# Three of four weight differences move from VectorE to GpSimd in the last feed-forward stage

## The chip, the cores and the metric

The kernel runs on one core of one Trainium2 chip. The metric is the device time of one execution in microseconds (us), the lower the better. It is taken several times, and the median counts.

## The reference, cut to what matters

The reference is a trunk of two layers over 512 tokens of width 1024, in f32. Each layer has a mixer (attention and two gated recurrences), cross-attention to a memory, and a gated feed-forward stage. Only the feed-forward stage of the second layer is touched by the change:

```python
def conv_glu_ffn(h_norm, w_in, conv_w, conv_b, w_out):
    gate, up = jnp.split(h_norm @ w_in, 2, axis=-1)   # w_in is 1024 x 5632
    ...                                               # causal conv of width 3 over the tokens of gate
    return (jax.nn.silu(conv) * up) @ w_out           # w_out is 2816 x 1024
```

## The kernel before

All products keep f32 accuracy by splitting both operands into a high and a low half (`hi` = the value rounded to fp32r, `lo` = the value minus `hi`), and by three matmuls for each product: hi x hi, hi x lo, lo x hi.

**Slabs.** Weights arrive as slabs of 128 x 1024 f32 (512 KB) in a ring of three raw buffers, loaded by SyncE's DMA queue in the order of use. ScalarE writes `w_hi` (L1356). The low half `w_lo` is made in one of three ways: a subtraction on GpSimd (L691), a subtraction on VectorE (`out_low`, L1940, for the slabs of the output product), or, for most `up` slabs of the last feed-forward stage, ScalarE writes the negated rounded slab into `w_lo` (L1355) and a DMA issued by GpSimd (L681) adds the raw slab onto it. `w_hi` and `w_lo` have three buffers each, so that slab k can be split only once TensorE has finished slab k-3. A raw buffer is loaded again once its slab's low half is made (SyncE waits for that).

**The last feed-forward stage.** The 22 chunks of 128 hidden columns come in three groups g of 8, 8 and 6 (`LG`). For each chunk c TensorE multiplies the slab `("gate", g, c)` and then the slab `("up", g, c)`, 24 matmuls each. VectorE takes them out of the banks (L2232 for gate, L2241 for up), does the convolution (L2234, L2236, L2237), multiplies (L2243), and prepares operands for the output product (L1947 to L1958). ScalarE does the SiLU (L1707) and high halves (L1714, L1719, L1722). ScalarE splits slabs two ahead: only after the high halves of chunk c (`pair_high_halves`) does it split the gate slab of chunk c+2, and then the up slab of chunk c+2.

**The output product** behind each group is Strassen's form with seven half-size products, which need four sums of the activations and four differences of quarters of the weights. The quarters `b11`, `b12`, `b22`, `b21` of `w_out` are loaded whole during the chunks, and the differences are

- `t1 = b12 - b11`, `t2 = b22 - t1`, `t3 = b22 - b12`, `t4 = b21 - t2`.

Each is one subtraction per slab of 128 x 1024 (two slabs per group; the second slab of the last group is 128 x 512): 24 subtractions in all, all on VectorE, at L1933 in `t_sum`. `T_CHUNK` says behind which chunk: for group 0 `t1`, `t2`, `t3` behind chunks 4, 5, 6, for group 1 behind 3, 4, 5, for group 2 behind 2, 3, 4. `t4` comes later. `t1` and `b21` of group 0 are written over `h`, so that they wait for semaphore `hk_evac` to reach 8, when ScalarE (L1737) has copied `h`, transposed, out of the banks in eight pieces; it does the last four of these copies in chunk 4, behind its split of the slabs of chunk 5.

**GpSimd's queue** in this stage holds, slab by slab in the order of use, the subtraction for each gate slab (L691) and the DMA for each up slab (L681; `added` leaves out only the first two up slabs of group 0 and the first of the others). It waits for nothing else:

```python
if gi in dma_los:
    pool.wait_ge(S["negated"], added.index(gi) + 1)
    pool.dma_start(w_lo[gi % SPLIT][:, 0:n], raw[ring_of[gi] % RAW][:, 0:n], accum_op=ALU.add
                   ).then_inc(lo_in[dma_los[gi][0]], 16)
    continue
```

TensorE's `use` of an up slab waits for that DMA's semaphore `lo_in`.

Of the kernel before, what the change touches and what calls it, by code (L numbers as in the profile page):

```python
# [27 lines left out]
def build_trunk(nc, A, out):  # L28
# [8 lines left out]
    ACT, ALU, AX = mybir.ActivationFunctionType, mybir.AluOpType, mybir.AxisListType  # L37
# [165 lines left out]
    def pair_slabs(g):  # L203

        return [(s, min(2, LG[g] // 2 - 2 * s)) for s in range((LG[g] // 2 + 1) // 2)]
# [19 lines left out]
    def slab_of(layer, name):  # L225
        return first_slab[layer] + layer_at[layer][name]
# [21 lines left out]

    def t_count(g, name, s):

        return sum(len(T_AT) * len(pair_slabs(j)) for j in range(g)) + T_AT[name] * len(pair_slabs(g)) + s + 1

    with ExitStack() as ctx:

# [107 lines left out]
        def b_slab(name, s, nk):  # L362
# [25 lines left out]
            proj_mm h_added mem_r memT_mm m_hi_done m_lo_done ckv_mm ckv_evac ck_ss ck_r ck_done ckT_mm ckT_evac  # L388
            cq_mm cq_evac cq_ss cq_r cqT_mm cqT_evac
            ffn_mm gate_ready sg_done sg_scaled cig_half silu_done act_ready a_hi_done a_lo_done first_rest_in first_hi zeroed qx_done q_scaled  # L390
            p_hi_done p_lo_done sums_done t_done out_lo out_mm c_added
            nope_in sq_done tab_done kr_done constants_made bounds_done pos_in logits_in mix_rows_in rows_in pairs_made  angles_done tables_done""".split()
        S = {n: ctx.enter_context(nc.semaphore(n)) for n in names}
        raw_in = [ctx.enter_context(nc.semaphore(f"raw_in{i}")) for i in range(RAW)]
# [107 lines left out]
        with nc.Block() as block:  # L502
# [121 lines left out]
            def recurrences(pool, layer):  # L624
# [15 lines left out]
                for n in range(NT):  # L640
                    sg = sg_tok[:, n, :].rearrange("p (m h x) -> p m h x", m=2, x=64)
                    pool.tensor_tensor(sg, sg, spread[:, g0:g0 + 128].rearrange("p (m x) -> p m x", m=2).unsqueeze(2)
                                       .to_broadcast([P, 2, NH, 64]), ALU.mult).then_inc(S["sg_scaled"], 1)

            @block.gpsimd
            def _(pool):
                link = chain(pool, S["chain_p"])
# [26 lines left out]
                for layer in range(DEPTH):  # L674
                    for i, (nk, cols, src) in enumerate(layer_slabs[layer]):
# [9 lines left out]
                        if gi == 0:  # L685
# [4 lines left out]
                        pool.wait_ge(S["hi_split"], gi + 1)  # L690
                        pool.tensor_tensor(w_lo[gi % SPLIT][:, c0:n], whole[:, c0:n],  # L691
                                           w_hi[gi % SPLIT][:, c0:n].bitcast(f32), ALU.subtract).then_inc(S["lo_split"], 1)
                        if 2 <= gi < 2 + len(LEVELS):
                            pairs_of(gi - 2)
                        if i == SPLIT - 1:
# [618 lines left out]
            def _(act_):  # L1314
# [20 lines left out]
                for layer in range(DEPTH):  # L1335
                    def split_through(i):

                        while nsplit[0] <= min(i, len(flat) - 1):
                            k = nsplit[0]
                            nk, cols, src = flat[k]  # L1340
                            n = nk * cols
                            if k in ring_of:
                                whole = raw[ring_of[k] % RAW][:, 0:n]
                                act_.wait_ge(raw_in[ring_of[k] % RAW], arrivals[k])
                            else:
                                name, g, s = src
                                whole = b_slab(name, s, nk)
                                if name in T_AT:
                                    act_.wait_ge(S["t_done"], t_count(g, name, s))
                                else:  # L1350
                                    act_.wait_ge(b_in[name], b_loads(g))
                            if k >= SPLIT:
                                act_.wait_ge(*released[k - SPLIT])
                            if k in dma_los:
                                act_.activation(w_lo[k % SPLIT][:, 0:n], whole, ACT.Copy, scale=-1.0).then_inc(S["negated"], 1)  # L1355
                            act_.activation(w_hi[k % SPLIT][:, 0:n], whole, ACT.Copy).then_inc(S["hi_split"], 1)  # L1356
                            nsplit[0] += 1
# [410 lines left out]
            def _(dve):  # L1768
# [50 lines left out]
                for layer in range(DEPTH):  # L1819
# [90 lines left out]
                    def b_ready(g, name):  # L1910
                        dve.wait_ge(b_in[name], b_loads(g))

                    def t_sum(g, name, s, nk):

                        if name == "t1":
                            b_ready(g, "b11")
                            b_ready(g, "b12")
                            if g == 0:
                                dve.wait_ge(S["hk_evac"], 2 * NT)
                            plus, minus = "b12", "b11"  # L1920
                        if name == "t2":
                            b_ready(g, "b22")
                            dve.wait_ge(S["t_done"], t_count(g, "t1", s))
                            plus, minus = "b22", "t1"
                        if name == "t3":
                            dve.wait_ge(S["t_done"], t_count(g, "t1", s))
                            plus, minus = "b22", "b12"
                        if name == "t4":
                            b_ready(g, "b21")
                            dve.wait_ge(S["out_lo"], out_los[slab_of(layer, ("out", g, 0, s))])  # L1930
                            dve.wait_ge(S["t_done"], t_count(g, "t2", s))
                            plus, minus = "b21", "t2"
                        dve.tensor_tensor(b_slab(name, s, nk), b_slab(plus, s, nk), b_slab(minus, s, nk), ALU.subtract  # L1933
                                          ).then_inc(S["t_done"], 1)

                    def out_low(g, q, s, nk):

# [28 lines left out]
                    def out_stage(g):  # L1966

                        some = pair_slabs(g)
                        for q in range(len(PRODUCTS)):
                            add_product(g, q)  # L1970
                            if q + 2 < len(PRODUCTS):
                                for s, nk in some:
                                    out_low(g, q + 2, s, nk)
                            if q == 0:
                                for s, nk in some[1:]:
                                    t_sum(g, "t4", s, nk)

                    link(dve.tensor_scalar(lb_floor[:, :], lb_all[:, :, layer:layer + 1].squeeze(2), 1.0, None, ALU.mult))
                    link(dve.tensor_scalar(lb_rest[:, :], lb_floor[:, :], -1.0, 1.0, ALU.mult, ALU.add))
# [265 lines left out]
                    if layer == LAST:  # L2245
                        for g in range(len(LG)):
                            for c in range(LG[g]):
                                n = LG_FIRST[g] + c
                                some = pair_slabs(g)

                                def second_slab_low():
                                    for s, nk in some[1:]:
                                        out_low(g, 0, s, nk)

                                if c < LG[g] - 1:
                                    glu_chunk(n, 2 * (n % 2))
                                else:
                                    glu_chunk(n, 2 * (n % 2), second_slab_low)
                                pair_operands(g, c)
                                if c in T_CHUNK[g]:  # L2260
                                    for s, nk in some:
                                        t_sum(g, T_CHUNK[g][c], s, nk)
                                if c == LG[g] - 2:
                                    out_low(g, 0, *some[0])
                                    t_sum(g, "t4", *some[0])
                            out_stage(g)
                        continue

# [36 lines left out]
```

## Time and profile before

| | |
|---|---|
| median of 3 runs | 1407.16 us (1406.26 to 1407.54) |
| the profiled execution's own time | 1407.03 us |
| its span, first to last instruction | 1405.2 us |
| granted TensorE clock, mean | 0.996 |
| TensorE busy | 1386.0 us (99% of the span) |
| VectorE busy | 850.2 us (61%) |
| ScalarE busy | 666.1 us (47%) |
| GpSimd busy | 588.3 us (42%) |
| last feed-forward stage, chunks and output products | from about 1060 us of the span to its end |

The span leaves out 1.8 us of the execution's own time. Times in the trace's views are microseconds from the start of the span. In a list of instructions in order of time a row is: start, duration, engine, line, operation, output and inputs with shapes, count, and in brackets how long the engine had been idle and for whom it waited. PE is TensorE, DVE VectorE, ACT ScalarE, POOL GpSimd.

### The profile page before, as it was taken

Reading aid. Unit: us, or ns where it says so; the run is one execution under the profiler, and the core shown is the slowest. Engines: PE = TensorE matmul, PEld = TensorE weight load, DVE = VectorE, ACT = ScalarE, POOL = GpSimd, SP = SyncE. Lnnn points to the kernel's source line nnn. Section 1 sums busy time; section 2 is a strip of 40 time slices with the busy share of each in tenths; the row PEclk is TensorE's granted clock in tenths of the full one; section 3 lists DMA queues with packets and bytes.
Section 4 is the critical chain, followed back from the end, with each engine's and each line's share of the span. In section 5 each row is a group of like instructions: output and inputs, shape, how many; then the busy total and the mean of one; then the engine's idle time right before and its main releaser. Section 6 shows DMA issues by size and latency. Waiting matters only on the chain. (4 is left out here: it accounts for less than half of the span.)

```text
span 1405.2 us, 17641 instructions
## 1 busy us (share of the span) xinstructions
PE 1386.0 (99%) x6797; PEld 1137.1 (81%) x6797; DVE 850.2 (61%) x1267; ACT 666.1 (47%) x1127; POOL 588.3 (42%) x347
## 2 busy tenths in 40 slices
PE   8999999999999999999999999999999999999998
PEld 6888778887788888888888887788878878888887
DVE  4584675565775305664164656746657695598487
ACT  6747482655432212233256465736655443444333
POOL 5645663552444444444445457635423202220320
PEclk9999999999999999999999999999999999999999
DMA  6332012331243333332333220123326626651631
GB/s 179 96 100 61 30 37 80 110 108 58 76 119 91 97 98 99 97 105 83 103 96 95 84 76 16 46 75 121 105 57 189 165 53 188 151 126 60 165 90 60
DMA packets 178898, 135.11 MB, mean 96 GB/s; under 512 B 14945, under 2 KB 152960, under 8 KB 178816
## 3 DMA queue, kind: packets, MB, share of 16 engines
q1 hardware_dynamic: 175664, 124.55, 29.9%
q0 software_dynamic: 2592, 9.44, 3.4%
q8 instruction: 54, 0.88, 0.3%
q14 instruction: 28, 0.23, 0.1%
q10 hardware_dynamic: 560, 0.01, 0.0%
HBM read 122.44 MB, written 2.10 MB: 89 GB/s over the span
## 5 line engine op out<-in xcount | busy, mean ns | idle before, releaser
L691 POOL TENSOR_TENSOR w_lo<-raw,w_hi 128x1024 fp32r<-128x1024 f32 (+3 forms) x188 | 451.2, 2404 | 682.1 <-ACT w_hi L1356 680.4
L771 PE MATMUL bank<-x_hi,w_hi 128*128 128x512 f32 x944 | 371.5, 394 | 4.3 <-issue 1.7
L775 PE MATMUL bank<-x_hi,w_lo 128*128 128x512 f32 x944 | 367.5, 389 | 0.0
L773 PE MATMUL bank<-x_lo,w_hi 128*128 128x512 f32 x944 | 367.4, 389 | 0.0
L1356 ACT ACTIVATE w_hi<-raw 128x1024 fp32r<-128x1024 f32 (+2 forms) x205 | 212.8, 1039 | 217.4 <-PE bank L775 212.5
L771 PEld LDWEIGHTS bank<-x_hi,w_hi 128*128 128x128 f32 x944 | 177.2, 188 | 47.8 <-issue 8.6
L773 PEld LDWEIGHTS bank<-x_lo,w_hi 128*128 128x128 f32 x944 | 177.3, 188 | 37.5 <-issue 1.4
L775 PEld LDWEIGHTS bank<-x_hi,w_lo 128*128 128x128 f32 x944 | 177.2, 188 | 37.1
L1889 DVE TENSOR_TENSOR h<-h,bank 128x512 f32<-128x512 f32 x48 | 31.8, 682 | 105.2 <-PE bank L775 105.1
L1707 ACT ACTIVATE conv<-conv 128x512 f32<-128x512 f32 x44 | 27.8, 633 | 137.5 <-DVE conv L2237 137.5
L1822 DVE SCALAR_TENSOR_TENSOR x_lo<-h,gains_all,x_hi 128x512 fp32r<-128x512 f32 x40 | 41.9, 1059 | 64.1 <-ACT x_hi L1373 63.1
L2232 DVE TENSOR_TENSOR gate_in<-bank,r_bc 128x512 f32<-128x512 f32 x44 | 30.3, 689 | 80.5 <-PE bank L775 71.0
L771 PE MATMUL bank<-w_hi,x_hi 128*128 128x512 f32 (+1 forms) x192 | 77.9, 406 | 0.0
L2236 DVE SCALAR_TENSOR_TENSOR conv<-gate_in,gains_all,conv 128x512 f32<-128x512 f32 x44 | 76.6, 1742 | 1.6
L775 PE MATMUL bank<-w_hi,x_lo 128*128 128x512 f32 (+1 forms) x192 | 74.6, 389 | 0.0
L773 PE MATMUL bank<-w_lo,x_hi 128*128 128x512 f32 (+1 forms) x192 | 74.6, 388 | 0.0
L771 PE MATMUL bank<-a_hi,w_hi 128*128 128x512 f32 x176 | 68.5, 389 | 0.0
L773 PE MATMUL bank<-a_lo,w_hi 128*128 128x512 f32 x176 | 68.5, 389 | 0.0
L775 PE MATMUL bank<-a_hi,w_lo 128*128 128x512 f32 x176 | 68.5, 389 | 0.0
L771 PE MATMUL bank<-w_hi,p_hi 128*128 128x512 f32 x154 | 60.1, 390 | 0.9 <-DVE w_lo L1940 0.9
L775 PE MATMUL bank<-w_hi,p_lo 128*128 128x512 f32 x154 | 59.9, 389 | 0.0
L773 PE MATMUL bank<-w_lo,p_hi 128*128 128x512 f32 x154 | 59.9, 389 | 0.0
(343 smaller groups left out, 2482.1 us busy)
## 6 DMA issues: line engine op xcount, KB each, us to landing
raw<-in_w_ffn_in SPq DMA_DIRECT2D x88, 512.0 KB, 3.8
raw<-in_w_in SPq DMA_DIRECT2D x27, 512.0 KB, 3.8
raw<-in_w_ffn_out SPq DMA_DIRECT2D x20, 512.0 KB, 3.7
w_lo<-raw POOLq DMA_DIRECT2D x18, 512.0 KB, 7.0
raw<-in_w_mix_out SPq DMA_DIRECT2D x16, 512.0 KB, 3.9
raw<-in_w_ca_kv SPq DMA_DIRECT2D x32, 256.0 KB, 3.2
raw<-in_w_ca_q SPq DMA_DIRECT2D x8, 512.0 KB, 3.4
raw<-in_w_ca_out SPq DMA_DIRECT2D x8, 512.0 KB, 3.7
```

Of the source, the lines that this page charges most:

```text
L691: pool.tensor_tensor(w_lo[gi % SPLIT][:, c0:n], whole[:, c0:n], w_hi[gi % SPLIT][:, c0:n].bitcast(f32), ALU.subtract).then_inc(S["lo_split ...
L771: pe.matmul(o, ah, bh, start=first, stop=False, skip_group_check=shared_bank)
L773: pe.matmul(o, ah, bl, start=False, stop=False, skip_group_check=shared_bank)
L775: mm = pe.matmul(o, al, bh, start=False, stop=last, skip_group_check=shared_bank)
L1356: act_.activation(w_hi[k % SPLIT][:, 0:n], whole, ACT.Copy).then_inc(S["hi_split"], 1)
L1707: act_.activation(conv[n % 2][:, :], conv[n % 2][:, :], ACT.Silu).then_inc(S["silu_done"], 1)
L1822: dve.scalar_tensor_tensor(x_lo[:, k, :], h[:, k, :], gain_of(layer + w // 3, name, k), x_hi[:, k, :].bitcast(f32), ALU.mult, ALU.subtract ...
L1889: dve.tensor_tensor(h[:, k, :], h[:, k, :], pb[PROJ_BANKS[base // H_ADDS][half][c]][:, :], ALU.add).then_inc(S["h_added"], 1)
L2232: dve.tensor_tensor(gi[:, CONV - 1:], pb[b][:, :], r_bc[:, :], ALU.mult).then_inc(S["gate_ready"], 1)
L2236: link(dve.scalar_tensor_tensor(cv[:, :], gi[:, t:t + SEQ], w_(t), cv[:, :], ALU.mult, ALU.add))
```

## The change

`t1`, `t2` and `t3` are taken out of VectorE's program and put into GpSimd's, in the loop over the slabs, behind the subtraction for the gate slab of the chunk after the one where VectorE did them: for group 0 gate slabs 5, 6, 7, for group 1 gate slabs 4, 5, 6, for group 2 gate slabs 3, 4, 5. They stand ahead of the DMA of the up slab of the same chunk. That is 18 subtractions. `t4` stays on VectorE and has a semaphore of its own, `t4_done`. For groups 1 and 2 `t1` has a new wait, for the last `out_low` of the group before.

```diff
     def t_count(g, name, s):
-        return sum(len(T_AT) * len(pair_slabs(j)) for j in range(g)) + T_AT[name] * len(pair_slabs(g)) + s + 1
+        kinds = 1 if name == "t4" else 3
+        return sum(kinds * len(pair_slabs(j)) for j in range(g)) + T_AT[name] % 3 * len(pair_slabs(g)) + s + 1
...
+            def difference(pool, g, name, s, nk):
+                plus, minus = {"t1": ("b12", "b11"), "t2": ("b22", "t1"), "t3": ("b22", "b12")}[name]
+                if name == "t1":
+                    pool.wait_ge(b_in["b11"], b_loads(g))
+                    pool.wait_ge(b_in["b12"], b_loads(g))
+                    if g:
+                        pool.wait_ge(S["out_lo"], out_los[slab_of(LAST, ("out", g - 1, 6, pair_slabs(g - 1)[-1][0]))])
+                    else:
+                        pool.wait_ge(S["hk_evac"], 2 * NT)
+                else:
+                    pool.wait_ge(b_in["b22"], b_loads(g))
+                    pool.wait_ge(S["t_done"], t_count(g, "t1", s))
+                pool.tensor_tensor(b_slab(name, s, nk), b_slab(plus, s, nk), b_slab(minus, s, nk), ALU.subtract).then_inc(S["t_done"], 1)
...
             def _(pool):
...
                         pool.tensor_tensor(w_lo[gi % SPLIT][:, c0:n], whole[:, c0:n],
                                            w_hi[gi % SPLIT][:, c0:n].bitcast(f32), ALU.subtract).then_inc(S["lo_split"], 1)
+                        if layer == LAST:
+                            for g in range(len(LG)):
+                                for c, name in T_CHUNK[g].items():
+                                    if i == layer_at[LAST]["gate", g, c + 1]:
+                                        for s, nk_b in pair_slabs(g):
+                                            difference(pool, g, name, s, nk_b)
...
                                 pair_operands(g, c)
-                                if c in T_CHUNK[g]:
-                                    for s, nk in some:
-                                        t_sum(g, T_CHUNK[g][c], s, nk)
                                 if c == LG[g] - 2:
                                     out_low(g, 0, *some[0])
-                                    t_sum(g, "t4", *some[0])
+                                    last_difference(g, *some[0])
```

`last_difference` is the `t4` branch of `t_sum`, with `t4_done` in place of `t_done`; ScalarE waits for `t4_done` ahead of the high half of a `t4` slab.

## Rows read from the trace of the kernel before

**Rows 1.** The page: busy time, share of the span and instructions of TensorE and the others.

```profile
PE 1386.0 (99%) x6797; PEld 1137.1 (81%) x6797; DVE 850.2 (61%) x1267; ACT 666.1 (47%) x1127; POOL 588.3 (42%) x347
```

**Rows 2.** Waits of TensorE, 1050 to 1405 (total, times, longest us); last row 1125 to 1130.

```profile
PE bank L771 <- DMA w_lo<-raw: 1.3, 2, 1.0
PE bank L771 <- DVE w_lo L1940: 0.9, 2, 0.6
...
PE bank L771 <- DMA w_lo<-raw: 0.3, 1, 0.3
```

**Rows 3.** Line L1933: VectorE's t1, t2 and t3 (duration ns min/median/max, first and last start).

```profile
L1933 DVE TENSOR_TENSOR h<-b_y,b_x x6: 1211/1217/3439, 1112.3 to 1343.1; 128x1024 f32<-128x1024 f32 x5, 128x512 f32<-128x512 f32 x1
L1933 DVE TENSOR_TENSOR b_u<-b_z,h x6: 679/2318/3437, 1126.2 to 1359.1; 128x1024 f32<-128x1024 f32 x5, 128x512 f32<-128x512 f32 x1
L1933 DVE TENSOR_TENSOR b_y<-b_z,b_y x6: 687/1218/3434, 1135.8 to 1365.9; 128x1024 f32<-128x1024 f32 x5, 128x512 f32<-128x512 f32 x1
```

**Rows 4.** VectorE in order of time: evacuations of gate (L2232) and up (L2241) slabs.

```profile
1104.60 0.69 DVE L2232 TENSOR_TENSOR gate_in<-bank,r_bc 128x512 f32<-128x512 f32 x1 [2.01 <-PE bank L775]
...
1110.04 0.69 DVE L2241 TENSOR_TENSOR act<-bank,r_bc 128x512 f32<-128x512 f32 x1 [2.59 <-PE bank L775]
...
1115.48 0.69 DVE L2232 TENSOR_TENSOR gate_in<-bank,r_bc 128x512 f32<-128x512 f32 x1 [0.84 <-PE bank L775]
...
1214.58 0.69 DVE L2241 TENSOR_TENSOR act<-bank,r_bc 128x512 f32<-128x512 f32 x1 [1.53 <-PE bank L775]
...
1225.46 0.69 DVE L2241 TENSOR_TENSOR act<-bank,r_bc 128x512 f32<-128x512 f32 x1 [2.59 <-PE bank L775]
```

**Rows 5.** GpSimd in order of time: gate slabs 5, 6 of group 0; 4, 5 of group 1.

```profile
1102.30 2.55 POOL L691 TENSOR_TENSOR w_lo<-raw,w_hi 128x1024 fp32r<-128x1024 f32 x1 [9.31 <-ACT w_hi L1356]
1106.10 0.90 POOL L681 DMA_DIRECT2D w_lo<-raw  x1 [1.25 <-ACT w_lo L1355]
1117.57 2.39 POOL L691 TENSOR_TENSOR w_lo<-raw,w_hi 128x1024 fp32r<-128x1024 f32 x1 [10.57 <-ACT w_hi L1356]
1120.48 0.88 POOL L681 DMA_DIRECT2D w_lo<-raw  x1 [0.52 <-ACT w_lo L1355]
...
1217.49 2.38 POOL L691 TENSOR_TENSOR w_lo<-raw,w_hi 128x1024 fp32r<-128x1024 f32 x1 [5.48 <-ACT w_hi L1356]
1221.52 0.88 POOL L681 DMA_DIRECT2D w_lo<-raw  x1 [1.64 <-ACT w_lo L1355]
1230.39 2.56 POOL L691 TENSOR_TENSOR w_lo<-raw,w_hi 128x1024 fp32r<-128x1024 f32 x1 [8.00 <-ACT w_hi L1356]
1232.91 0.86 POOL L681 DMA_DIRECT2D w_lo<-raw  x1
```

**Rows 6.** L681, issue to landing: all 18; then those issued at 1221.5, 1232.9, 1358.0.

```profile
DMA to landing us min/median/max: 4.5/7.0/8.9
...
DMA to landing us min/median/max: 5.6/5.6/5.6
...
DMA to landing us min/median/max: 7.1/7.1/7.1
...
DMA to landing us min/median/max: 4.5/4.5/4.5
```

**Rows 7.** ScalarE in order of time: the last `hk_evac` copies, gate slab 6 of group 0.

```profile
1106.57 2.04 ACT L1737 ACTIVATE h_tok<-bank 128x512 f32<-128x512 f32 x4
...
1116.42 1.06 ACT L1356 ACTIVATE w_hi<-raw 128x1024 fp32r<-128x1024 f32 x1 [4.51 <-DMA raw<-in_w_ffn_in]
```

**Rows 8.** VectorE's convolution step alone, then beside a GpSimd subtraction; both engines near 278.

```profile
1105.91 0.75 DVE L2236 SCALAR_TENSOR_TENSOR conv<-gate_in,gains_all,conv 128x512 f32<-128x512 f32 x1
...
1117.58 2.94 DVE L2237 SCALAR_TENSOR_TENSOR conv<-gate_in,gains_all,conv 128x512 f32<-128x512 f32 x1
...
277.92 6.21 POOL L691 TENSOR_TENSOR w_lo<-raw,w_hi 128x1024 fp32r<-128x1024 f32 x2 [3.08 <-ACT w_hi L1356]
...
278.55 3.31 DVE L1831 TENSOR_TENSOR h_sq<-h_sq 128x1024 f32<-128x1024 f32 x1
```

More of the change, by code:

```diff
@@ L390, in build_trunk @@
             ffn_mm gate_ready sg_done sg_scaled cig_half silu_done act_ready a_hi_done a_lo_done first_rest_in first_hi zeroed qx_done q_scaled
-            p_hi_done p_lo_done sums_done t_done out_lo out_mm c_added
+            p_hi_done p_lo_done sums_done t_done t4_done out_lo out_mm c_added
             nope_in sq_done tab_done kr_done constants_made bounds_done pos_in logits_in mix_rows_in rows_in pairs_made  angles_done tables_done""".split()
@@ L1348, in split_through @@
                                 if name in T_AT:
-                                    act_.wait_ge(S["t_done"], t_count(g, name, s))
+                                    act_.wait_ge(S["t4_done" if name == "t4" else "t_done"], t_count(g, name, s))
                                 else:
@@ L1911, in b_ready, with last_difference @@
                         dve.wait_ge(b_in[name], b_loads(g))
[L1913 to L1934, printed above, removed]
+                    def last_difference(g, s, nk):
+                        b_ready(g, "b21")
+                        dve.wait_ge(S["out_lo"], out_los[slab_of(layer, ("out", g, 0, s))])
+                        dve.wait_ge(S["t_done"], t_count(g, "t2", s))
+                        dve.tensor_tensor(b_slab("t4", s, nk), b_slab("b21", s, nk), b_slab("t2", s, nk), ALU.subtract
+                                          ).then_inc(S["t4_done"], 1)
                     def out_low(g, q, s, nk):
@@ L1975, in out_stage @@
                                 for s, nk in some[1:]:
-                                    t_sum(g, "t4", s, nk)
+                                    last_difference(g, s, nk)
                     link(dve.tensor_scalar(lb_floor[:, :], lb_all[:, :, layer:layer + 1].squeeze(2), 1.0, None, ALU.mult))
```

## The prediction

> **What bounds the kernel now.** I read the page first, for who is busy. TensorE is busy 99% of the span, the other engines 42 to 61% [rows 1], so taking work from VectorE gains only what TensorE now waits for. The waits of TensorE in the last feed-forward stage give the size: 1.3 us for the DMA that makes an up slab's low half, 0.9 us for VectorE's `out_low` [rows 2]. That is 2.2 us in 350. The question is then how much slack the low halves have on the way through GpSimd's queue.
>
> For that I read VectorE, GpSimd and ScalarE in order of time. Each evacuation marks the end of a slab on TensorE: gate slab 4 of group 0 at 1104.6, up slab 4 at 1110.0, gate slab 5 at 1115.5 [rows 4], so a slab takes 5.44 us. GpSimd makes the low half of gate slab 5 at 1102.30 to 1104.85 and issues the DMA for up slab 5 at 1106.10 [rows 5]. Such a DMA lands 4.5 to 8.9 us after issue, median 7.0 [rows 6]. One of the TensorE waits, 0.3 us, stands just where up slab 6 of group 0 begins [rows 2]: this chain already touches TensorE.
>
> **What is removed.** 18 VectorE subtractions. The full ones take 1.21 us undisturbed and up to 3.44 us [rows 3]. VectorE gets 5 to 10 us less per group. The most that this can give back on TensorE is the 0.9 us of waits for `out_low`, of which 0.6 us lie behind the last up slab, at the end of a chain that starts with that slab's own evacuation and holds no t-difference; I take 0.3 us, between 0 and 0.9.
>
> **What is added on GpSimd.** A subtraction of this shape costs 2.39 us there [rows 5]; two make 4.8 us. They stand between the gate slab's subtraction and the up slab's DMA, and the queue is in order, so the DMA moves back by 4.8 us less the time that GpSimd sits idle in between. Behind the DMA waits TensorE. Behind the landing waits also SyncE, which reloads the raw buffer, two slabs further on; that has some 5 us to spare and is costed at nothing (its cover gone, the next gate slab would be late by what is missing).
>
> How late is the landing? I count from the end E of the up slab two chunks back. ScalarE splits gate slab k behind the high halves of chunk k-2, which are more work for odd k. GpSimd is through with an even gate slab at 1219.87, 5.3 us behind E = 1214.58, and with an odd one at 1232.95, 7.5 us behind E = 1225.46 [rows 4, 5]. TensorE needs up slab k three slabs behind E, at +16.3 us.
>
> What does the DMA take when it goes out later? Its landing follows the raw loads that run beside it: 7.1 us where it goes out with the subtraction's end, which also frees a raw buffer; 5.6 us where it goes out 1.6 us later; 4.5 us for the last one, with no raw load left [rows 5, 6]. Delayed by 4.8 us it should meet little traffic: I take 5.0 us, bounds 4.5 and 7.0.
>
> - Even k: 5.3 + 4.8 + 5.0 = 15.1, under 16.3: no stall. By 7.0 us it would be 0.8 us.
> - Odd k: 7.5 + 4.8 + 5.0 = 17.3, a stall of 1.0 us; by 4.5 us 0.5, by 7.0 us 3.0.
>
> **Both engines together.** VectorE's convolution step takes 0.75 us alone and 2.94 us when it starts with a GpSimd subtraction; it ends 0.6 us behind it [rows 8]. Near 278 us two GpSimd subtractions, worth 4.8 us, take 6.2 us because a VectorE operation slips in between, and that one takes 3.3 us [rows 8]. So they exclude each other both ways. The differences will now run during the convolution of the chunk before. Each lets one VectorE operation of 0.55 to 0.75 us in, and the convolution, and with it ScalarE's next gate split, comes about 1.1 us later (one convolution step waits for the second difference's end). Of this nothing is in the trace of before, so it is an estimate from those rows, with 0 and 2.4 us as bounds. I add 0.3 to 0.5 us for each pair of differences, and 1.1 us for the late split where the chunk before had differences too.
>
> The Trainium skill ("SBUF — State Buffer", section "SBUF: two separate sides") has the same exclusion as a lock that the first comer holds for the whole instruction. The skill's "DMA: Bandwidth & Descriptors" (section "Anatomy of one DMA — SWDGE (gpsimd) path") puts a DMA from GpSimd at 2.0 us plus bytes / 436e3, an estimate of 3.2 us for 512 KB; by it the odd slabs would not stall (7.5 + 4.8 + 3.2 = 15.5) and only the first term of the sum below would be left, at 1.3 us. The trace disagrees: none of the 18 took under 4.5 us [rows 6].
>
> **Group 0 is worse.** `t1` waits for `hk_evac`, whose last copy ends at 1106.57 + 2.04 = 1108.61 [rows 7]. On VectorE nobody minded, since its turn came at 1112 [rows 3]. GpSimd gets there at 1104.85 and stands until 1108.61, with the DMA of up slab 5 behind it. Then 4.8 us and about 0.2 us for VectorE's operations: issue at 1113.7 in place of 1106.10. Raw loads are thick there (ScalarE waits 4.5 us for one until 1116.42 [rows 7]), so I take the median of 7.0 us: landing at 1120.7, TensorE needs it at 1115.5. Stall 5.2 us; by 4.5 us it is 2.7, by 8.9 us 7.1.
>
> **The sum.**
>
> - Group 0: up slab 5 5.2 us. Up slab 6: TensorE is now 5.2 us later, its DMA at 1119.96 + 4.8 = 1124.8 lands at 1130 and TensorE comes at 1131.6: none, and the 0.3 us of before goes. Up slab 7 (odd): 1.0 + 0.3 = 1.3 us.
> - Group 1: up slab 4 (even) none. Slab 5: 1.0 + 0.3 + 1.1 = 2.4 us. Slab 6 even, and the stall of slab 5 lies ahead of it: none.
> - Group 2: slab 3 (odd) 1.0 + 0.5 = 1.5 us. Slab 4 none. Slab 5: the second slab is half, so 3.7 us in place of 4.8, and no raw loads: 7.5 + 1.1 + 3.7 + 0.4 + 4.5 = 17.2, 0.9 us.
> - Sum 5.2 + 1.3 + 2.4 + 1.5 + 0.9 = 11.3, less 0.3 and 0.3: **10.7 us**.
>
> The profiled execution took 1407.03 us, its span 1405.2, so the 1.8 us around it stay; it agrees with the median 1407.16 within 0.13 us. Forecast 1407.2 + 10.7: **1418 us**.
>
> **Rivals.**
>
> 1. *The DMAs land fast and nothing interferes.* 4.5 us each, no 1.1 us, no slips: group 0 2.6 + 0.5, group 1 0.5, group 2 0.5 (its slab 5 comes to 15.7, no stall), sum 4.1 less 0.6, so 1410.7 us. For it: the quiet row of 4.5 us. Against it: raw loads are never quite absent. Chance 0.15.
> 2. *Every difference costs its full 4.8 us or more.* Landings stay at 7.0 us (8.9 for the first), with the exclusion as above: 7.1, 3.3, 4.4, 3.5, 3.4 in the order of the sum, together 21.7 less 0.6, even slabs absorbed by the stall ahead of them: 1428 us. For it: the median of all landings. Against it: the order of landings by traffic. Chance 0.12.
> 3. *The other side: VectorE's relief decides.* If the differences fitted into GpSimd's idle time, only TensorE's waits could go: at most 1.3 + 0.9 = 2.2 us, 1405.0 us. It decides only if an odd slab's DMA lands within 16.3 - 7.5 - 4.8 = 4.0 us, and up slab 5 of group 0 within 1.8 us. For it: GpSimd idles most of each chunk, and its subtraction waits 8 us for ScalarE [rows 5]. Against it: the idle time lies ahead of the gate slab's subtraction, not behind it. Chance 0.04, of which a gain over 0.2% (2.8 us, about what a measurement of this kernel can tell from no change) is 0.02.
> 4. *No difference:* gains and stalls cancel, for instance if stalls of group 0 stay near 2.6 us and the others vanish. 1407 to 1410 us. Chance 0.06.
>
> The forecast's own case (1412 to 1424) has 0.63. The range reaches from the fast landings to most of the way to rival 2: 1410 to 1426. Faster 0.02, same 0.08, slower 0.90.
>
> **What the profile after would show.** TensorE's waits for the DMA of `w_lo` grow from 1.3 us to about 11, one of some 5 us near 1115 to 1121, the others of 1 to 2 us at odd up slabs, the next group's clear of them. GpSimd shows 18 subtractions on a new line, 2.4 us each, the first at 1108.6, and up-slab DMAs issued right behind a pair. VectorE's convolution steps lengthen beside them. The landing times of these DMAs drop towards 5 us. I would be wrong if the first `t1` did not start at 1108.6, if landings stayed at 7 us (then slower), or if ScalarE's splits came so much earlier with VectorE relieved that odd gate slabs were through well before +7.5 us (then less slow).

## The result and the profile after

The changed kernel takes 1418.11 us (median of 4 runs, 1417.62 to 1419.52), the kernel before, run beside it, 1406.71 us. The ratio is 1.0084, with a 95% interval of 1.0069 to 1.0099: slower by 9.7 to 13.9 us. The profiled execution has a span of 1415.9 us, 10.7 more than before. A kernel's own runs differ by some 4 us, and this goes with the clock granted to TensorE: of the runs of the kernel before that stood beside the experiments, the 11 with a mean granted clock of 0.999 took 1404.3 to 1405.9 us, the seven with 0.995 took 1407.6 to 1409.8 us.

Below, a pair is the two subtractions of one of `t1`, `t2`, `t3`, for its two slabs. The port stands for whatever it is that VectorE and GpSimd can't hold at the same time.

The page, as in [rows 1]: TensorE is busy for 1.3 us more with the same 6797 matmuls, VectorE has 18 instructions fewer and is busy for 2.9 us *more*, GpSimd has 18 more and 42 us more.

```profile
PE 1387.3 (98%) x6797; PEld 1136.1 (80%) x6797; DVE 853.1 (60%) x1249; ACT 665.9 (47%) x1127; POOL 630.6 (45%) x365
```

The waits of TensorE from 1050 us on (total, times, longest), which answer to [rows 2], then the same view of the six stretches in which the new ones lie (1110 to 1120, 1130 to 1145, 1240 to 1250, 1260 to 1275, 1352 to 1365, 1365 to 1380):

```profile
PE bank L793 <- DMA w_lo<-raw: 8.9, 6, 4.3
PE bank L793 <- ACT w_hi L1378: 1.3, 1, 1.3
PE bank L793 <- DVE w_lo L1947: 0.5, 1, 0.5
...
PE bank L793 <- DMA w_lo<-raw: 4.3, 1, 4.3
PE bank L793 <- ACT w_hi L1378: 1.3, 1, 1.3
PE bank L793 <- DMA w_lo<-raw: 2.0, 1, 2.0
PE bank L793 <- DMA w_lo<-raw: 0.8, 1, 0.8
PE bank L793 <- DMA w_lo<-raw: 0.7, 1, 0.7
PE bank L793 <- DMA w_lo<-raw: 0.2, 1, 0.2
```

They belong to up slabs 5 and 7 of group 0, 5 and 7 of group 1, 3 and 5 of group 2. The other two waits, 0.9 us for a DMA near 1100 and 0.5 us for `out_low` near 1390, had their like before the change (1.0 and 0.6 us). The 1.3 us is put down to ScalarE, whose `w_hi` had ended 10 us earlier; the same instruction waits for the DMA too, and that landed 4.5 us behind its issue at 1138.97, at 1143.5, as TensorE went on at 1143.76. In all 10.7 us of waits against 2.2 before: 8.5 of the 10.7 us.

GpSimd in order of time, groups 0 and 1 (as [rows 5]). `t1` begins at 1107.83, having waited 3.94 us for the copies of `h`, and the DMA for up slab 5, issued at 1106.10 before, goes out at 1112.97:

```profile
1101.35 2.54 POOL L707 TENSOR_TENSOR w_lo<-raw,w_hi 128x1024 fp32r<-128x1024 f32 x1 [9.31 <-ACT w_hi L1378]
1107.83 5.19 POOL L659 TENSOR_TENSOR h<-b_y,b_x 128x1024 f32<-128x1024 f32 x2 [3.94 <-ACT h_tok L1759]
1112.97 0.89 POOL L697 DMA_DIRECT2D w_lo<-raw  x1
...
1236.75 2.56 POOL L707 TENSOR_TENSOR w_lo<-raw,w_hi 128x1024 fp32r<-128x1024 f32 x1 [5.50 <-ACT w_hi L1378]
1239.28 5.36 POOL L659 TENSOR_TENSOR b_u<-b_z,h 128x1024 f32<-128x1024 f32 x2
1244.59 0.87 POOL L697 DMA_DIRECT2D w_lo<-raw  x1
```

The DMAs behind a pair land sooner than before, as [rows 6] led to expect: 5.6 us for up slab 5 of group 0, then 4.5 to 5.0 us for the other eight. In the stretches of these eight the core's DMA engines moved 106 to 120 GB/s, which is about this transfer's own 512 KB (estimated from 512 KB in 4.5 us: 116 GB/s); beside the 5.6 us they moved 220 GB/s.

The remaining time is in this list of TensorE, behind the wait of 4.3 us. The matmuls start 0.43 us apart until 1122.55, then 0.23 us apart:

```profile
1118.83 0.51 PE L793 MATMUL bank<-x_hi,w_hi 128*128 128x512 f32 x1 [4.34 <-DMA w_lo<-raw]
1119.14 0.63 PE L795 MATMUL bank<-x_lo,w_hi 128*128 128x512 f32 x1
...
1122.12 0.59 PE L797 MATMUL bank<-x_hi,w_lo 128*128 128x512 f32 x1
1122.55 0.39 PE L793 MATMUL bank<-x_hi,w_hi 128*128 128x512 f32 x1
1122.78 0.39 PE L795 MATMUL bank<-x_lo,w_hi 128*128 128x512 f32 x1
```

The rows by stretch, around the wait and behind it. Behind the length they give the busy time of TensorE, its weight loads, VectorE, ScalarE and GpSimd, each with its count, then the granted clock, the DMA share and GB/s:

```profile
1114.50:1119.50 5.00, 0.67 (x2) 0.62 (x3) 4.86 (x4) 3.06 (x3) 3.70 (x2) 0.96 0.72 152
1119.50:1121.00 1.50, 1.50 (x5) 1.14 (x4) 1.50 (x1) 0.00 (x0) 1.50 (x2) 0.50 0.67 197
```

The clock was at its lower level, 1.2 in place of 2.4 GHz, for 3.4 us: about 1.7 us lost, mostly in the eight intervals of 0.43. The waits of 2.0 us and less show nothing of the kind in this execution; in other kernels some do, as e4 shows. With it 8.5 + 1.7 = 10.2 of the 10.7 us are placed; the rest is some 0.1 us at each restart and less than the runs differ by.

VectorE's convolution beside a pair, in group 1, answers to [rows 8]. Each of three steps takes until GpSimd's instruction beside it is over (the gate slab's subtraction, then the two of the pair) and gets in behind it:

```profile
1237.68 1.92 DVE L2241 TENSOR_SCALAR conv<-gate_in,gains_all 128x512 f32<-128x512 f32 x1
1239.63 2.76 DVE L2243 SCALAR_TENSOR_TENSOR conv<-gate_in,gains_all,conv 128x512 f32<-128x512 f32 x1
1242.42 2.76 DVE L2244 SCALAR_TENSOR_TENSOR conv<-gate_in,gains_all,conv 128x512 f32<-128x512 f32 x1
```

That is why VectorE is busy for longer with less work: its time in the list includes what it stands before the port. In the last stage its three convolution lines take 84.0 us in place of 50.7, which is 33 us more, and the 18 subtractions that left had taken 33 us, part of it before the port too.

### The profile page after: what moved, and what is told of

Its sections match the earlier page's. It is cut to its first block, busy times and chain, and to the rows that moved or that the text cites. A ratio compares the mean times of both kernels' runs of the same rounds, so it can differ in the third digit from the quotient of the medians.

```text
span 1415.9 us, 17647 instructions
## 1 busy us (share of the span) xinstructions
PE 1387.3 (98%) x6797; PEld 1136.1 (80%) x6797; DVE 853.1 (60%) x1249; ACT 665.9 (47%) x1127; POOL 630.6 (45%) x365
## 4 chain that ended last, share of the span: by engine, by line
PE 87%; DVE 5%; DMA 2%; ACT 2%; issue 2%; POOL 1%; SPq 0%; DVEq 0%; POOLq 0%; ACTq 0%
PE bank L793 25%; PE bank L797 25%; PE bank L795 25%; PE bank L967 2%; DMA w_lo<-raw 2%; PE bank L1096 1%; PE bank L1097 1%; PE bank L955 1%; PE bank L1176 1%; PE bank L1136 1%; POOL h L659 1%; DVE Q L2125 1%; DVE conv L2243 1%; PE bank L1251 1%; PE bank L1075 1%
## 5 line engine op out<-in xcount | busy, mean ns | idle before, releaser
L2243 DVE SCALAR_TENSOR_TENSOR conv<-gate_in,gains_all,conv 128x512 f32<-128x512 f32 x44 | 92.8, 2109 | 1.6
```

The source lines that it names most:

```text
L2243: link(dve.scalar_tensor_tensor(cv[:, :], gi[:, t:t + SEQ], w_(t), cv[:, :], ALU.mult, ALU.add))
```

## The experiments

Eleven kernels. All times are compared with the kernel before, run on the same chip: 1407.05 us for e1 to e4, 1406.16 us for e5 to e8, 1405.91 us for e9 to e11. In e5, e7, e8 and e11 the differences on VectorE and on GpSimd count on separate semaphores. A difference in median of 2 to 3 us between two of the slower kernels is at the edge of what the runs can tell; where the intervals of the ratios overlap, the text says so and the traces have to decide.

**e1: the pairs behind the up slab's DMA.**

```diff
-                        if layer == LAST:
-                            ...
-                                    if i == layer_at[LAST]["gate", g, c + 1]:
                         if gi in dma_los:
                             ...
                             pool.dma_start(w_lo[gi % SPLIT][:, 0:n], ..., accum_op=ALU.add
                                            ).then_inc(lo_in[dma_los[gi][0]], 16)
+                            for g in range(len(LG)):
+                                for c, name in T_CHUNK[g].items():
+                                    if i == layer_at[LAST]["up", g, c + 1]:
+                                        for s, nk_b in pair_slabs(g):
+                                            difference(pool, g, name, s, nk_b)
                             continue
```

> The 18 subtractions stay on GpSimd, but each pair stands behind the DMA of the up slab of the same chunk, not ahead of it. Theory (the loss is the place in GpSimd's queue, ahead of a DMA that TensorE waits for): in the trace of before GpSimd is idle for 8 us from an odd chunk's DMA to the next gate slab, so a pair of 4.8 us fits and no up slab's DMA is late. TensorE's waits in the stage fall back from 10.7 us to some 2 us and the time to 1405 to 1409 us. Rival (the loss is the exclusion of VectorE and GpSimd, which makes convolutions and ScalarE's splits late wherever the pairs stand): the waits stay above 6 us and the time at 1413 us or more.

Measured: 1422.18 us, ratio 1.0106 (1.0091 to 1.0121), which is no less than the changed kernel (the intervals overlap). The theory that the place in the queue is the whole loss falls. GpSimd and VectorE in order of time in group 1:

```profile
1238.14 0.87 POOL L697 DMA_DIRECT2D w_lo<-raw  x1
1238.76 5.03 POOL L659 TENSOR_TENSOR b_u<-b_z,h 128x1024 f32<-128x1024 f32 x2
...
1238.52 5.83 DVE L2242 SCALAR_TENSOR_TENSOR conv<-gate_in,gains_all,conv 128x512 f32<-128x512 f32 x1
```

TensorE's waits in the stage (total, times, longest):

```profile
PE bank L792 <- DMA w_lo<-raw: 7.4, 6, 1.9
PE bank L792 <- DVE w_lo L1946: 5.3, 4, 2.8
```

The DMA goes out right behind the gate slab's subtraction, and GpSimd is through with each pair 3.8 us or more before its next gate slab is there to be split, so its queue holds nothing up. But a convolution step that takes 0.75 us alone takes 5.83 us: it stands before the port for both subtractions, not for one. So the SiLU, the product, ScalarE's high halves and its next split are late, chunk by chunk, and so the DMAs again, and VectorE is 2.8 us late with `out_low` at the last output product. TensorE also waits 1.6 us at gate slab 7 of group 1, whose low half ends at 1264.9, just before TensorE goes on at 1265.0; the view names no releaser for it. These waits come to 14.3 us against 2.2 before. The last of the DMA waits, 1.9 us, has the clock at 0.50 behind it for 3.4 us.

One pair of e1 begins later than its DMA, `t1` of group 0, since it waits for the copies of `h`. There VectorE gets in at the boundary: its step stands for the second subtraction alone.

```profile
1104.38 0.90 POOL L697 DMA_DIRECT2D w_lo<-raw  x1 [1.25 <-ACT w_lo L1376]
1107.08 5.20 POOL L659 TENSOR_TENSOR h<-b_y,b_x 128x1024 f32<-128x1024 f32 x2 [1.80 <-ACT h_tok L1758]
...
1110.06 2.51 DVE L1959 TENSOR_TENSOR s_tmp<-act 128x256 f32<-128x256 f32 x1
```

**e2: matmuls that fill the long wait.**

```diff
+                                if n == 5:
+                                    pe.wait_ge(S["hk_evac"], 2 * NT)
+                                    for _ in range(18):
+                                        pe.matmul(pb[7][:, :], x_hi[:, 0, 0:P], x_hi[:, 0, :], start=True, stop=True)
                                 feature_chunk(("up", g, c), b + 1, 2, S["ffn_mm"], evacs[1])
```

> The changed kernel with 18 matmuls of 128 x 512, whose result nobody reads, on TensorE ahead of up slab 5 of group 0, where it waits 4.3 us for the DMA; they take 18 x 0.227 = 4.1 us. Theory (after the long wait the granted clock is 0.5 for some 3.7 us and the next nine matmuls cost 0.2 us more each, 1.8 us): the clock stays at 1.0, these nine run at 0.227 us apart, and the time falls by 1.8 us, to 1416.3 us. Rival (the nine matmuls were slow for another reason, such as the heavy DMA traffic at that moment): they stay slow and the time stays at 1418 us, or rises by what the fillers overrun.

Measured: 1415.64 us, ratio 1.0066 (1.0054 to 1.0079), 2.5 us under the changed kernel by the medians; the intervals overlap, and the profiled execution is 1.1 us shorter. TensorE's list: the fillers (18 matmuls that nobody needs) take 4.24 us, a wait of 1.2 us is left, since this time the DMA took 6.6 us to land, and the matmuls behind it are 0.23 us apart.

```profile
1115.03 4.24 PE L1314 MATMUL bank<-x_hi 128*128 128x512 f32 x18
1120.49 0.47 PE L793 MATMUL bank<-x_hi,w_hi 128*128 128x512 f32 x1 [1.22 <-DMA w_lo<-raw]
1120.80 0.39 PE L795 MATMUL bank<-x_lo,w_hi 128*128 128x512 f32 x1
```

The granted clock stays at 1.00 in the row of 1120 to 1122 and in those around it. The slow matmuls go with the idle time and not with the DMA traffic, as the theory said. That useless work made the whole kernel faster is likely, by its trace and its medians, but not shown clear of the spread.

**e3: `t1` of group 0 back on VectorE, behind chunk 4.** The loop in GpSimd's program skips `(0, "t1")`, and VectorE's has it again:

```diff
+                                if c in T_CHUNK[g] and (g, T_CHUNK[g][c]) in ON_VECTOR:
+                                    for s, nk in some:
+                                        difference(dve, g, T_CHUNK[g][c], s, nk)
```

> The changed kernel with t1 of group 0 alone back on VectorE behind chunk 4; 16 subtractions stay on GpSimd. Theory (t1's wait for the copies of h and its 5.1 us hold up the DMA of up slab 5; the stall there, 4.5 us and 1.8 us of slow clock, shields up slab 6, whose own DMA goes out 4.8 us later than before and had no slack): the wait at up slab 5 goes, 6.3 us, but one of some 3.5 us (4.5 to 5.5 with a slow clock behind it) appears at up slab 6, and takes the 1.5 us at up slab 7 with it. Net gain 2.5 to 4.5 us: 1413.5 to 1415.5 us. Rival (each stall stands by itself, so that the stall of slab 5 is simply saved): 1411.8 us.

Measured: 1415.61 us, ratio 1.0063 (1.005 to 1.0075), 2.5 us under the changed kernel by the medians (the intervals overlap). The wait at up slab 5 is gone and one of 4.1 us stands at up slab 6, from 1126.9 to 1131.0, again with the clock at 0.50 behind it; the one at slab 7 is gone. The time came out at the slow end of the theory's range. So the largest stall of the changed kernel shielded another that is nearly as long. The row of TensorE's waits in the stretch from 1125 to 1135:

```profile
PE bank L795 <- DMA w_lo<-raw: 4.1, 1, 4.1
```

**e4: all of group 0 back on VectorE** (`ON_VECTOR` holds `t1`, `t2` and `t3` of group 0).

> All three differences of group 0 back on VectorE, those of groups 1 and 2 on GpSimd as in the changed kernel. Theory (the loss of each group is its own late DMAs; in the profile after, groups 1 and 2 hold 2.2, 1.0, 0.9 and 0.5 us of it): 4.5 us over the kernel before, 1411.2 us, waits at the same slabs. Rival (lateness carries from group 0 into the later ones): under 3 us over it, at most 1409.7 us.

Measured: 1410.82 us, ratio 1.0027 (1.0016 to 1.0039), 3.8 us over the kernel before (2.3 to 5.5). The trace has a wait of 2.0 us for a DMA at up slab 5 of group 1 and three of 0.5 us in group 2, two for DMAs and one for VectorE's `out_low`. The waits stand at the same slabs as in the changed kernel, as the theory said; the time alone would not exclude the rival's 3 us. By the medians groups 1 and 2 cost about 4 us, group 0 about 7 or 8.

This execution, the slowest of the six, shows something else: behind the wait of 2.0 us, which ends at 1243.96, the clock falls for 3.4 us and matmuls start 0.43 us apart, where the same wait in the changed kernel had nothing behind it. The row by stretch, in the columns given above:

```profile
1245.00:1248.00 3.00, 3.00 (x9) 2.34 (x7) 2.96 (x2) 0.00 (x0) 3.00 (x3) 0.50 0.86 254
```

So 1.6 us of this execution's loss is the clock's.

**e5: one subtraction at a time, in VectorE's pauses.** Group 0 on VectorE. In groups 1 and 2 GpSimd does one subtraction behind an up slab's DMA (two behind the last of group 2), and first waits for the convolution that VectorE is at:

```diff
+                        # behind pool.dma_start for the up slab of chunk at[0]
+                        if how == "hole":
+                            pool.wait_ge(S["silu_done"], past(LAST, "silu_done") + 2 * (LG_FIRST[g] + at[0] - 1) + 1)
+                        difference(pool, g, name, s, dict(pair_slabs(g))[s])
```

> Group 0's differences are back on VectorE. Those of groups 1 and 2 stay on GpSimd, one subtraction of 2.4 us at a time behind an up slab's DMA, and each waits until VectorE has ended the convolution of the chunk that TensorE is at; VectorE then has nothing to do for some 3 us. Theory after e1 (two causes: a late DMA where the pair stands ahead of it, a late convolution where it runs beside one): with neither, the cost is gone, TensorE's waits in the stage are 2.5 us or less, 1405.5 to 1408 us. Rival (GpSimd's work in these chunks costs time wherever it stands, by memory traffic or its DMA's descriptors): 1409 us or more.

Measured: 1406.56 us, ratio 0.9999 (0.999 to 1.0007). Twelve of the 18 subtractions are on GpSimd; each of 128 x 1024 takes its 2.39 us, and VectorE's steps just ahead of it stay at 0.75 us.

```profile
1221.92 0.88 POOL L713 DMA_DIRECT2D w_lo<-raw  x1 [1.55 <-ACT w_lo L1391]
1223.36 2.39 POOL L667 TENSOR_TENSOR b_u<-b_z,h 128x1024 f32<-128x1024 f32 x1 [0.56 <-DVE conv L2259]
...
1222.52 0.75 DVE L2259 SCALAR_TENSOR_TENSOR conv<-gate_in,gains_all,conv 128x512 f32<-128x512 f32 x1
```

Neither cause, no cost; and no gain. TensorE's waits in the stage are 3.4 us, more than the 2.5 expected; none of them lies in group 1, and the only one in group 2 is 0.5 us for `out_low`.

**e6: e1 with each subtraction cut in two.**

```diff
-                pool.tensor_tensor(b_slab(name, s, nk), b_slab(plus, s, nk), b_slab(minus, s, nk), ALU.subtract).then_inc(S["t_done"], 1)
+                parts = [[b_slab(x, s, nk)[:, c:c + nk * HALF // 2] for x in (name, plus, minus)] for c in (0, nk * HALF // 2)]
+                for d, p, m in parts:
+                    ins = pool.tensor_tensor(d, p, m, ALU.subtract)
+                ins.then_inc(S["t_done"], 1)
```

> The kernel of e1, pairs behind the up slab's DMA, with each GpSimd subtraction cut in two of 128 x 512 (four of some 1.25 us in a row in place of two of 2.4). In e1 a convolution step on VectorE waited 5.6 to 5.9 us for both subtractions. Theory (the port is given anew at each instruction, and VectorE's waiting step gets it at the next boundary that it is in time for): the step ends after 2 to 3 us, TensorE's waits fall and the time comes to 1416 us or less. Rival (GpSimd keeps the port as long as its next instruction stands ready): the step still takes 5.5 us or more, the time stays within 2 us of e1's 1422 us.

Measured: 1423.58 us, ratio 1.0123 (1.0107 to 1.0138). The rival's numbers come out: the step stands for all four. Its reason, that GpSimd keeps the port as long as its next instruction is ready, is not what e9 shows.

```profile
1239.92 0.88 POOL L700 DMA_DIRECT2D w_lo<-raw  x1
1240.53 5.31 POOL L661 TENSOR_TENSOR b_u<-b_z,h 128x512 f32<-128x512 f32 x4
...
1240.30 6.10 DVE L2245 SCALAR_TENSOR_TENSOR conv<-gate_in,gains_all,conv 128x512 f32<-128x512 f32 x1
```

**e7: one of each pair.** The first slab's subtraction on GpSimd behind the gate slab's, as in the changed kernel, the second on VectorE; `t1` of group 0 all on VectorE.

> Of each pair only the first slab's subtraction is on GpSimd, where the change put it, the second on VectorE where it was; t1 of group 0 is all on VectorE. 8 subtractions of 2.4 us moved, none that waits for the copies of h. Theory (an up slab's DMA has slack, some 1.8 us behind odd gate slabs with a landing of 7.1 us, and the landing gets shorter as the DMA goes out later, so that 2.5 us fit and 5.1 do not): groups 1 and 2 wait at most 1 us together; in group 0 up slab 6, which had no slack, costs 1 us. 1407 to 1409 us. Rival (cost in proportion to what is moved): half of the 7.6 us that all but t1 of group 0 costs (e3's 1415.6 less the kernel before, less 1.0), some 1411 us.

Measured: 1406.24 us, ratio 0.9999 (0.999 to 1.0008). Waits for the up slabs' DMAs: 0.7 us at slab 3 of group 0, as before the change, and 1.2 us at slab 6; none in groups 1 and 2. Eight of the 18 subtractions, late by one instruction each, cost nothing that 11 runs show, a little less than the theory's 1407 us. The cost is not in proportion to what is moved: it starts where the slack ends.

**e8: `t1` of group 0 alone on GpSimd.**

> Only t1 of group 0 is on GpSimd, the other 16 subtractions on VectorE as in the kernel before. Theory (t1 waits for the copies of h until they end and then takes 5.1 us, and up slab 5's DMA behind it is late): one wait of 4.3 us at up slab 5 with nine slow matmuls behind it, 1.8 us, and the 0.3 us of before at up slab 6 gone; 1412.3 to 1413.3 us. Rival (in the changed kernel the stall at slab 5 needs the other differences too): under 1411 us.

Measured: 1410.85 us, ratio 1.0035 (1.0022 to 1.0047), 4.7 us over the kernel before (3.1 to 6.6). The time alone speaks for the rival: it lies below the theory's 1412.3 us and just inside the rival's range. The trace speaks for the theory: a wait of 4.28 us at up slab 5 and slow matmuls behind it, from the fifth on, with seven intervals of 0.43 us and a shorter one at each end, 1.6 us. So the stall needs none of the other differences; the theory's size was too large, or the five runs lie low.

```profile
1112.07 0.39 PE L810 MATMUL bank<-x_hi,w_lo 128*128 128x512 f32 x1
1116.73 0.47 PE L806 MATMUL bank<-x_hi,w_hi 128*128 128x512 f32 x1 [4.28 <-DMA w_lo<-raw]
...
1118.12 0.63 PE L810 MATMUL bank<-x_hi,w_lo 128*128 128x512 f32 x1
```

**e9: the changed kernel with each subtraction cut in two** (e6's cut, in the place of the change).

> The changed kernel (pairs behind the gate slab's subtraction) with each GpSimd subtraction cut in two of 128 x 512. In the changed kernel a convolution step of VectorE got the port at the boundary between two subtractions (2.77 us a step), in e1 and e6 it did not (5.6 to 6.1 us). Theory A (GpSimd keeps the port over a row of instructions only when its DMA issue stands just ahead of them): here VectorE gets in at each boundary, a convolution step beside the row takes 1.4 to 1.7 us, GpSimd's row grows to some 6 us; time within 2 us of the changed kernel's 1418 us. Theory B (instructions of 128 x 512 in a row leave no gap wherever they stand): a step takes 5 us or more and the time rises to 1420 us or more.

Measured: 1419.21 us, ratio 1.0092 (1.0078 to 1.0106). Theory A holds: VectorE gets in at each boundary, with steps of 1.66 us. And one chunk of the same kernel shows its other side: where the gate slab's subtraction comes 0.6 us behind a DMA issue with the row of four behind it, VectorE stays out for all.

```profile
1237.69 2.57 POOL L710 TENSOR_TENSOR w_lo<-raw,w_hi 128x1024 fp32r<-128x1024 f32 x1 [3.60 <-ACT w_hi L1381]
1240.22 6.58 POOL L661 TENSOR_TENSOR b_u<-b_z,h 128x512 f32<-128x512 f32 x4
1246.73 0.89 POOL L700 DMA_DIRECT2D w_lo<-raw  x1
1247.34 2.69 POOL L710 TENSOR_TENSOR w_lo<-raw,w_hi 128x1024 fp32r<-128x1024 f32 x1
1249.69 5.28 POOL L661 TENSOR_TENSOR b_y<-b_z,b_y 128x512 f32<-128x512 f32 x4
...
1240.57 1.67 DVE L2246 SCALAR_TENSOR_TENSOR conv<-gate_in,gains_all,conv 128x512 f32<-128x512 f32 x1
...
1249.94 5.32 DVE L2244 TENSOR_SCALAR conv<-gate_in,gains_all 128x512 f32<-128x512 f32 x1
```

**e10: e1 with a gap between the two of a pair.**

```diff
+                if s:
+                    pool.wait_ge(S["t_done"], t_count(g, name, s) - 1)
                 pool.tensor_tensor(b_slab(name, s, nk), b_slab(plus, s, nk), b_slab(minus, s, nk), ALU.subtract).then_inc(S["t_done"], 1)
```

> The kernel of e1 (pairs behind the up slab's DMA), and the second subtraction of each pair waits on a semaphore for the end of the first. Theory (VectorE's step is kept out only because the next GpSimd instruction stands ready at the boundary): the step gets the port there and takes some 3 us in place of 5.7, each convolution is 2.5 us less late, ScalarE's splits too, and the time falls from 1422 us to 1410 to 1415 us. Rival (a waiting VectorE step is served only once GpSimd has been idle for longer, or the DMA's descriptors hold the port): the step keeps its 5.6 us and the time stays at 1420 to 1423 us.

Measured: 1419.16 us, ratio 1.0088 (1.0074 to 1.0102), 3 us under e1 by the medians, with intervals that overlap, and between the theory's range and the rival's. The step beside the pair takes 3.48 us in place of 5.83: the mechanism is right, a gap of 0.17 us lets VectorE in. The size was not: the next step then stands for the second subtraction (2.77 us), so that the convolution is late by 4.7 us all told against 5.1 in e1, and the waits for `out_low` are still 4.4 us.

```profile
1238.15 2.68 POOL L661 TENSOR_TENSOR b_u<-b_z,h 128x1024 f32<-128x1024 f32 x1
1241.00 2.64 POOL L661 TENSOR_TENSOR b_u<-b_z,h 128x1024 f32<-128x1024 f32 x1 [0.17 <-POOL b_u L661]
...
1237.90 3.48 DVE L2244 SCALAR_TENSOR_TENSOR conv<-gate_in,gains_all,conv 128x512 f32<-128x512 f32 x1
1241.42 2.77 DVE L2245 SCALAR_TENSOR_TENSOR conv<-gate_in,gains_all,conv 128x512 f32<-128x512 f32 x1
```

**e11: e5 with `t2` of group 0 too, in chunks 6 and 7.**

> The kernel of e5 (groups 1 and 2 on GpSimd, one subtraction per chunk behind the up slab's DMA and VectorE's convolution) with t2 of group 0 as well, in chunks 6 and 7; 14 of 18 subtractions on GpSimd. VectorE is 2.4 to 4.5 us less late ahead of group 0's output product, where e5 still waits 1.0 us for its out_low. Theory (with no late DMA and no late convolution nothing is lost, and there is hardly anything to gain, since all waits of the stage are some 2 to 3 us): 1404.5 to 1407.5 us, no difference from the kernel before that five rounds show. Rival (VectorE's relief pays where it is late): 1403.5 us or less.

Measured: 1406.13 us, ratio 1.0002 (0.9992 to 1.0011). Fourteen of the 18 subtractions are on GpSimd at no cost and no gain. The 1.0 us for `out_low` at the end of group 0, which e5 had, is gone, as was expected, and the wait near 1125 that the view puts down to ScalarE is 1.0 us in place of 0.7. No version that beats the kernel before was found; all its waits in the stage are 2.2 us, 0.16%.

## Why the prediction was right, and where it was not

The forecast of 1418 us met 1418.11. Its chain of causes holds for the changed kernel; the terms are less exact than the sum, and that the sum met the time to 0.2 us is luck: errors of up to 0.8 us in single terms cancel.

- **`t1` of group 0 waits for the copies of `h`.** Right: GpSimd stands for 3.94 us and e8 shows the stall by itself. The stall was put at 5.2 us. The wait is 4.3, because the landing took 5.6 us and not the median 7.0 that I took; and the clock's fall adds 1.7, which I did not foresee. The term is 6.0 us in place of 5.2.
- **Even slabs have room, odd ones not.** Right in its order. Up slab 7 of group 0: 1.3 us forecast, 1.3 measured. Group 1: slab 5 2.4 and 2.0, slabs 4 and 6 none and none. Group 2: slab 3 1.5 and 0.7, slab 5 0.9 and 0.2; these two terms were too large, and the landings, 5.0 and 4.6 us, were as taken. In slab 3 the pair was counted as two full subtractions, 4.8 + 0.5 us, though the second slab of group 2 is half as wide, as the term for slab 5 says; it took 4.28 us. In slab 5 the 1.1 us for a late split did not come: GpSimd was through with the gate slab 7.5 us behind the end of up slab 3 (1368.27 less 1360.78).
- **Landings get shorter as the DMA goes out later.** Right: 4.5 to 5.0 us for eight of nine, where 5.0 was taken. The estimate of 3.2 us by the Trainium skill's "DMA: Bandwidth & Descriptors" (section "Anatomy of one DMA — SWDGE (gpsimd) path") stays out of reach: none of the 18 in the changed kernel took under 4.5 us either.
- **Up slab 7 of group 1** has a wait of 0.8 us that I had at none. It has no differences of its own; its gate slab was split late behind a late convolution, and its DMA took 8.4 us. In e2, with the same differences, that DMA took 7.2 us and TensorE did not wait there, so this term comes and goes.
- **VectorE's relief** was put at 0.3 us on TensorE, and the waits for `out_low` fell from 0.9 to 0.5 us. That VectorE would have 5 to 10 us less per group was wrong: it is busy for 2.9 us more in all, because it stands before the port for about as long as the subtractions had taken.
- **Both engines together.** Priced at 0.3 to 0.5 us a pair and 1.1 us for a late split. In the changed kernel that is about right for group 1: GpSimd was through with gate slab 5 8.2 us behind the end of up slab 3 (1239.31 less 1231.1, estimated as gate slab 4's evacuation at 1225.66 and one slab of 5.44), where it was 7.5 before, and the pair took 5.36 us for 4.8. But I read the exclusion as a surcharge on the late DMA, and it is a cause of its own: e1 takes the lateness in the queue away and still loses 15 us, the clock's 1.7 us among them. e5 and e11, which remove both causes, and e7, which keeps both small, are back at the kernel before. The rivals' dividing line, a landing within 4.0 us, was therefore not the only way back: e7 stays under the slack by moving half.

The two causes do not add up. Stalls absorb each other: e3 takes 6 us of stall away and gains 2.5 by the medians, since the next slab's DMA was as late. e4 and e8 together (3.8 and 4.7 us) come to 8.5 of the 11.4 us; the other 3 us are left for `t2` and `t3` of group 0 beside `t1`. No run had these alone, and with intervals of 3 to 4 us on each of the terms the rest is not measured well.

What stays open is why a waiting VectorE step is kept out for a whole row of GpSimd instructions when a DMA issue stands just ahead of the row, and gets in at each boundary when it does not. The runs show only that it is so. `t1` of group 0 in e1, where the row begins 2.7 us behind the issue and VectorE gets in, points to the issue; but that row also starts after a wait of GpSimd for ScalarE, so that the issue itself is the cause is not shown.

## What to carry to other kernels

In this kernel the in-order queue that holds a transfer on TensorE's path had slack for one more instruction, not for two; count from the last release to the landing before putting work ahead of the transfer, and look for a wait that the new place makes the whole queue share. Moving work between VectorE and GpSimd moves it only if the two don't meet at the port: one GpSimd instruction at a time, started by a semaphore when VectorE pauses, was free here, a row of them was not. A stall that is removed is worth only what the next one behind it leaves. And a stall of TensorE can cost more than its length, by the clock behind it, so look at the granted clock in the rows behind each wait.

## What the runs showed of the hardware that was not expected

- A wait of 4.1 to 4.3 us on TensorE was followed by a stretch at the lower clock (granted clock 0.50) in the changed kernel, in e3, e8 and e9: seven to nine matmul intervals of 0.43 us in place of 0.23. In the first three it lasted 3.4 us and cost 1.6 to 1.7 us, in e9 6.8 us, of which 2.2 us fell on matmuls. With the wait filled by 18 useless matmuls (e2) it did not come.
- For shorter waits the length did not decide it. Waits of 2.0 us had none behind them in the changed kernel, e2 and e3, 2.4 and 2.5 us none in e9, 2.8 us none in e1; but 2.0 us in e4, 1.9 us in e1, 1.8 and 2.6 us in e10 and 2.8 us in e6 were followed by 3.4 us at 0.50. What decides between them the runs do not show.
- A VectorE step beside a row of GpSimd subtractions took 2.8 us where the row followed another GpSimd computation (one subtraction of 128 x 1024), 1.7 us with halves, but 4.7 to 6.1 us, the whole row, where a DMA issue of GpSimd had started 0.6 us ahead of it (e1, e6), or ahead of the gate slab's subtraction before it (one chunk of e9). In e1 itself, where `t1` of group 0 started 2.7 us behind the DMA issue, it was 2.5 us. A semaphore wait of 0.17 us inside the row brought it down to 3.5 us (e10). The Trainium skill's "SBUF — State Buffer" (section "SBUF: two separate sides") has the lock held for one instruction; that fits the first kind of row and not the second, and there the measurement decides.
- A DMA issued from GpSimd over 512 KB landed in 4.5 to 5.0 us where the core's DMA engines moved 106 to 120 GB/s, about what it moves itself, and in 5.3 to 8.4 us where they moved 127 to 260 GB/s (changed kernel).
